# A two-block transformer kernel: small transfers ahead of x, the narrow slab as stationary operand, and input slabs moved between the steps of two attentions

## What is computed

```python
# first block
mod = silu(c) @ w_ada + b_ada            # six vectors of 1024: shifts, scales, gates
h = modulate(rmsnorm(x, norm_mix_g), sh_m, sc_m)
q, k, v, qi, ki, wi, u, ga, gb = split(h @ w_in)    # ki has 64 columns, wi 8
# index scores from qi, ki, wi choose 64 keys for each query; attention over these;
# a gated causal convolution of u (31 taps, w_dw); both projected, gated, added; feed-forward
# second block
h = rmsnorm(x, norm_mix_g)
qa, ka, va, qb, kb, vb, ga, gb = split(h @ w_in_2)  # 512 columns each, ga and gb 1024
qa, ka = rope(qa), rope(ka)
ya = diff_attention(qa, ka, va, lam)     # 4 heads, two softmaxes, second subtracted with lam
yb = chunk_band_attention(qb, kb, vb, rel_bias)     # 8 heads
x = x + (sigmoid(ga) * (ya @ w_up_a) + sigmoid(gb) * (yb @ w_up_b)) @ w_out
# cross attention: q = h @ w_cq, k, v = split(rmsnorm(mem) @ w_ckv); then feed-forward
```

## Time and profile before

| | us |
|---|---|
| median of 3 runs | 979.19 (978.38 to 985.32) |
| the profiled execution | 981.8, its span 980.0 |
| TensorE busy | 932.3 (95%) |
| VectorE, ScalarE, GpSimd busy | 629.6, 458.5, 29.6 |

### The profile page before, as it was taken

The page is one execution under the profiler, slowest core; times in us unless marked ns, Lnnn a source line. Parts: engine busy times, 40 slices in busy tenths (PEclk is TensorE's granted clock), DMA queues, the critical chain, the costliest instruction groups (busy, mean ns, idle before and its releaser), DMA issues.

```text
span 980.0 us, 12127 instructions
## 1 busy us (share of the span) xinstructions
PE 932.3 (95%) x4313; PEld 749.4 (76%) x4313; DVE 629.6 (64%) x1020; ACT 458.5 (47%) x708; POOL 29.6 (3%) x41
## 2 busy tenths in 40 slices
PE   4799899999999999999999999999999999999997
PEld 4688664578878888887888777788788878888785
DVE  4478899988765555576766534578554565555444
ACT  1144432357364444453744554474455365555432
POOL 2100000000000000000000000000000000000000
PEclk9989999999999999999999999999999999999999
DMA  9977622584566565476565443146462456555531
GB/s 330 338 285 271 216 87 87 174 305 175 168 220 210 172 189 196 171 244 228 164 217 177 129 129 129 43 150 216 143 202 85 130 181 194 183 174 194 188 130 43
DMA packets 102999, 178.05 MB, mean 182 GB/s; under 512 B 6302, under 2 KB 52619, under 8 KB 102954
## 3 DMA queue, kind: packets, MB, share of 16 engines
q1 hardware_dynamic: 96138, 151.23, 46.9%
q0 software_dynamic: 6816, 26.22, 7.3%
HBM read 176.39 MB, written 1.05 MB: 181 GB/s over the span
## 4 chain that ended last, share of the span: by engine, by line
PE 81%; issue 7%; DVE 5%; DMA 3%; ACT 2%; SPq 0%; POOL 0%; DVEq 0%; POOLq 0%; ACTq 0%
PE bank L550 19%; PE bank L552 19%; PE bank L551 19%; PE bank L952 10%; PE bank L583 3%; DMA tap_rows<-in_w_dw 2%; DMA ada_raw<-in_w_ada 2%; PE bank L777 1%; ACT w_hi L1201 1%; DVE w_lo L1660 1%; PE bank L931 1%; PE bank L629 1%; PE bank L793 1%; PE bank L621 1%; PE bank L1146 1%
## 5 line engine op out<-in xcount | busy, mean ns | idle before, releaser
L1660 DVE TENSOR_TENSOR w_lo<-raw_weights,w_hi 128x1024 fp32r<-128x1024 f32 x267 | 324.4, 1222 | 241.5 <-ACT w_hi L1201 240.1
L1201 ACT ACTIVATE w_hi<-raw_weights 128x1024 fp32r<-128x1024 f32 x267 | 281.0, 1058 | 307.7 <-PE bank L552 230.0
L550 PE MATMUL bank<-w_hi,a_hi 128*128 128x512 f32 (+1 forms) x824 | 328.0, 398 | 5.9 <-DVE w_lo L1660 3.3
L552 PE MATMUL bank<-w_hi,a_lo 128*128 128x512 f32 (+1 forms) x824 | 321.0, 390 | 0.0
L551 PE MATMUL bank<-w_lo,a_hi 128*128 128x512 f32 (+1 forms) x824 | 320.6, 389 | 0.0
L550 PEld LDWEIGHTS bank<-w_hi,a_hi 128*128 128x128 f32 x824 | 155.6, 189 | 43.4 <-issue 7.3
L552 PEld LDWEIGHTS bank<-w_hi,a_lo 128*128 128x128 f32 x824 | 155.7, 189 | 32.7
L551 PEld LDWEIGHTS bank<-w_lo,a_hi 128*128 128x128 f32 x824 | 155.9, 189 | 29.9 <-issue 0.2
L952 PE MATMUL bank<-w_hi,ff_hi 128*128 128x512 f32 x176 | 55.1, 394 | 0.8 <-DVE hidden_rows L2162 0.5
L952 PE MATMUL bank<-w_lo,ff_hi 128*128 128x512 f32 x176 | 54.3, 389 | 0.0
L952 PE MATMUL bank<-w_hi,ff_lo 128*128 128x512 f32 x176 | 54.2, 389 | 0.0
(11 more groups left out here) (260 smaller groups left out, 867.4 us busy)
## 6 DMA issues: line engine op xcount, KB each, us to landing
raw_weights<-in_w_in SPq DMA_DIRECT2D x40, 1024.0 KB, 5.1
raw_weights<-in_w_ffn_in SPq DMA_DIRECT2D x44, 512.0 KB, 4.7
raw_weights<-in_w_gate_up SPq DMA_DIRECT2D x44, 512.0 KB, 4.3
ada_raw<-in_w_ada POOLq DMA_DIRECT2D x10, 1024.0 KB, 7.7
ada_start<-in_w_ada POOLq DMA_DIRECT2D x10, 1024.0 KB, 11.5
raw_weights<-in_w_ffn_out SPq DMA_DIRECT2D x9, 1024.0 KB, 4.9
raw_weights<-in_w_down SPq DMA_DIRECT2D x9, 1024.0 KB, 4.9
raw_weights<-in_w_out SPq DMA_DIRECT2D x8, 1024.0 KB, 5.1
```

Source lines behind the costliest of these rows:

```text
L550: pe.matmul(ps, hi[:, kt, ts], wh, start=start, stop=False)
L552: return pe.matmul(ps, lo[:, kt, ts], wh, start=False, stop=stop)
L1201: act.activation(w_hi[:, slot, 0:m], raw[:, b % RAW, half * PIECE:half * PIECE + m], ACT.Copy)\
L1660: dve.tensor_tensor(w_lo[:, slot, 0:m], raw[:, b % RAW, half * PIECE:half * PIECE + m], w_hi[:, slot, 0:m], ALU.subtract).then_inc(lo_read ...
```

## The change

SP issues the constants and the small vectors ahead of the wait and of x. TensorE transposes the vectors behind block 1's columns instead of behind the first sums; VectorE copies them behind block 2. The narrow slab's weights become the stationary operand (72 columns) and the rows the moving one (256 columns), so that ki comes out transposed: 24 matmuls. ScalarE evicts it into `kiT`, a DMA on POOL's queue doubles it, and wi is transposed back by TensorE (8 columns a tile). In the second block three slabs (QB, KB, VB) run before banded attention; QA, KA, VA and half of the memory keys run one piece a step in it, and the four gate slabs two pieces a step in differential attention, whose filler is gone. The piece now stands ahead of `d_turn`, ScalarE's eviction ahead of `d_exp`. Rope is cut into four parts in banded attention's steps, its transposes follow in steps 9, 10, 13 and 14, and the transposes of the second half of the memory keys move behind the first query slab. The diff, cut to its core:

```diff
-IN2_COLS = (E_QA, E_KA, E_QB, E_KB, E_VA, E_VB, E_GA, E_GA + W, E_GB, E_GB + W)
+IN2_COLS = (E_QB, E_KB, E_VB)
-MIXED = (("k", 1), ("a", 0), ("a", 1), ("b", 0), ("b", 1), ("v", 0))
-FILL2 = (1,) * 16 + (1, 0) * 4
-AHEAD2 = (0,) * 2 + (1,) * 13 + (0,) + (1, 0) * 3 + (1, 1)
+MIXED = (("h", E_QA), ("h", E_KA), ("h", E_VA), ("k", W), ("h", E_GA), ("h", E_GA + W), ("h", E_GB), ("h", E_GB + W),
+         ("v", 0))
+FILL2 = (1,) * 16 + (2,) * 8
+AHEAD2 = (0,) * 2 + (1,) * 14 + (2,) * 8
+ROPE_AT = {5: ((0, 0),), 6: ((0, 1), (0, 2)), 7: ((1, 0),), 8: ((1, 1), (1, 2)),
+           9: ((2, 0),), 10: ((2, 1), (2, 2)), 11: ((3, 0),), 12: ((3, 1), (3, 2))}
+TURN_AT = (9, 10, 13, 14)
...
-        sp.wait_ge(*ada_signal(1))
-        sp.dma_start(x[:], a["x"].rearrange("o (t p) d -> p (o t) d", p=P)).then_inc(sem["x_landed"], 16)
         early = cols["half"][1]
...
         sp.dma_start(tap_rows[:], a["w_dw"].rearrange("o t i c -> (o t i) c")).then_inc(small_landed, 16)
+        sp.wait_ge(*ada_signal(1))
+        sp.dma_start(x[:], a["x"].rearrange("o (t p) d -> p (o t) d", p=P)).then_inc(sem["x_landed"], 16)
...
-        for n in range(12, 20):
+        for n in range(12, 14):
+            ada_block(n)
+        pool.wait_ge(sem["wi_turned"], 1)
+        pool.dma_start(kiT[DH:2 * DH, :], kiT[0:DH, :]).then_inc(sem["ki_doubled"], 16)
+        for n in range(14, 20):
             ada_block(n)
...
-        for n in range(4):
+        for n in range(2):
             start_columns(n)
         pe.wait_ge(sem["const_landed"], 16)
-        start_sums(0)
-        start_sums(1)
...
         last.then_inc(sem["vec_turned"], 1)
+        for n in range(2, 4):
+            start_columns(n)
+        start_sums(0)
+        start_sums(1)
         hold(5, 0)
...
-        for t in range(TT):
-            for kt in range(KD):
-                last = mm3(bank[2 * (U_SMALL % 2) + t][:, 0:SMALL], kt, t, a_hi, a_lo, sm_hi[:, kt, :],
-                           sm_lo[:, kt, :], kt == 0, kt == KD - 1)
...
+        out = bank[2 * (U_SMALL % 2)][0:SMALL, 0:SEQ]
+        for kt in range(KD):
+            pe.matmul(out, sm_hi[:, kt, :], a_hi[:, kt, :], start=(kt == 0), stop=False)
+            before = pe.matmul(out, sm_lo[:, kt, :], a_hi[:, kt, :], start=False, stop=False)
+            last = pe.matmul(out, sm_hi[:, kt, :], a_lo[:, kt, :], start=False, stop=(kt == KD - 1))
...
+        slab(P_IN2, U_IN2, 0, N_M2)
+        for t in range(TT):
+            pe.wait_ge(acc_free[t], U_K0 + 1)
+        turn4(4, 0, k0_rows, sem["key_turned"])
+        slab(P_IN2 + 4, U_IN2 + 1)
+        for j in range(3):
+            piece(P_IN2 + 8 + j, U_IN2 + 2, j, 4)
+            if j == 0:
                 for t in range(TT):
-                    pe.wait_ge(acc_free[t], U_K0 + 1)
-                turn4(4, 0, k0_rows, sem["key_turned"])
...
+                    pe.wait_ge(acc_free[t], U_IN2 + 2)
                 pe.wait_ge(sem["key_copied"], 2)
...
         for n in range(len(DS)):
-            if n == 0:
-                hold(4, 6)
-            elif n % 2 == 0:
-                for _ in range(9):
-                    pe.matmul(bank[n // 6][:, 3 * P:4 * P], ident, ones, start=True, stop=True)
+            mixed_step(16 + n)
             d_turn(n)
             if n + 2 < len(DS):
                 d_scores(n + 2)
-            mixed_step(16 + n)
...
-        for s in range(2):
-            slab(P_CQ + 4 * s, U_CQ + s, 0, (N_CR) if s == 0 else None)
+        slab(P_CQ, U_CQ, 0, N_CR)
+        for t in range(TT):
+            pe.wait_ge(acc_free[t], U_IN2 + 7)
+        turn4(4, W, k_rows, sem["key_turned"])
+        slab(P_CQ + 4, U_CQ + 1)
...
             keys = P * (n % 2 + 1)
+            mixed_out(16 + n)
             if n + 1 < 8:
                 d_exp(n + 1)
-            mixed_out(16 + n)
             mixed_weights(16 + n)
...
-            elif n == 6:
+            elif n == 2:
                 dve.wait_ge(sem["vec_turned"], 1)
```

More of the change, by code:

```diff
@@ L454, in _ @@
             load(62 + j, slab_src(w2["w_ckv_2"], 4 * j, 0))
-        for s, c in enumerate(IN2_COLS[:6]):
+        for s, c in enumerate(IN2_COLS):
             for j in range(2):
                 load(64 + 2 * s + j, slab_src(w2["w_in_2"], 4 * j, c))
-        first = {"k": 0, "v": D, "a": E_GA, "b": E_GB}
         for m, (kind, c) in enumerate(MIXED):
             for j in range(2):
-                load(76 + 2 * m + j, slab_src(w2["w_ckv_2" if kind in "kv" else "w_in_2"], 4 * j, first[kind] + c * W))
+                load(70 + 2 * m + j, slab_src(w2["w_in_2" if kind == "h" else "w_ckv_2"], 4 * j, c + D * (kind == "v")))
         for n, name in ((88, "w_up_b_2"), (90, "w_up_a_2")):
@@ L1000, in _ @@
             piece(P_K0 + j, U_K0, j, 4, hi=mem_hi, lo=mem_lo, freed_by=(acc_free[0], U_K0))
-        for s in range(4):
-            slab(P_IN2 + 4 * s, U_IN2 + s, 0, N_M2 if s == 0 else None)
-            if s == 1:
-                for t in range(TT):
-                    pe.wait_ge(acc_free[t], U_K0 + 1)
-                turn4(4, 0, k0_rows, sem["key_turned"])
-        for j in range(4):
-            piece(P_IN2 + 16 + j, U_IN2 + 4, j, 4)
-            if j == 1:
-                pe.wait_ge(sem["key_copied"], 2)
[L1011 to L1018, removed]
+        slab(P_IN2, U_IN2, 0, N_M2)
[6 more added lines that the diff above has]
+            if j == 0:
+                for t in range(TT):
+                    pe.wait_ge(acc_free[t], U_IN2 + 2)
+                pe.wait_ge(sem["key_copied"], 2)
                 turn4(4, E_QB, z, sem["t2"])
                 turn4(6, E_KB, z, sem["t2"])
-        pe.wait_ge(sem["t2_copied_act"], 4)
-        pe.wait_ge(sem["t2_copied_dve"], 4)
+        pe.wait_ge(sem["t2_copied_act"], 2)
+        pe.wait_ge(sem["t2_copied_dve"], 2)
         def last_input_piece(scores):
@@ L1027, in last_input_piece @@
             scores(1)
-            piece(P_IN2 + 23, U_IN2 + 5, 3, 4)
+            piece(P_IN2 + 11, U_IN2 + 2, 3, 4)
         def mixed_piece(j):
-            hi, lo = (mem_hi, mem_lo) if MIXED[j // 4][0] in "kv" else (a_hi, a_lo)
-            piece(P_IN2 + 24 + j, U_IN2 + 6 + j // 4, j % 4, 4, pair=1, hi=hi, lo=lo)
+            hi, lo = (a_hi, a_lo) if MIXED[j // 4][0] == "h" else (mem_hi, mem_lo)
+            piece(P_IN2 + 12 + j, U_IN2 + 3 + j // 4, j % 4, 4, pair=1, hi=hi, lo=lo)
         def mixed_step(n):
@@ L1296, in project_slabs @@
                 for k in range(4):
-                    if s == 5 and k == 3:
+                    if s == 2 and k == 3:
                         softmax_exp("b_", 0)
@@ L1333, in _ @@
         for t in range(TT):
-            act.wait_ge(*((piece_used, P_SMALL + 1) if t else (acc_done, U_SMALL + 1)))
-            act.activation(z[:, t, C_KI:C_U], bank[2 * (U_SMALL % 2) + t][:, 0:SMALL], ACT.Copy)\
+            act.wait_ge(piece_used, P_SMALL + 1)
+            act.activation(kiT[0:SMALL, t * P:(t + 1) * P], bank[2 * (U_SMALL % 2)][0:SMALL, t * P:(t + 1) * P], ACT.Copy)\
                 .then_inc(acc_free[t], 1)
@@ L2341, in _ @@
                               ALU.mult).then_inc(acc_free[1], 1)
+            if s == 0:
+                for g in (2, 3):
+                    copy_pair(sem["key_turned"], g + 1, mem_kT[:, 2 * g:2 * g + 2, :], 2 + g, sem["key_copied"])
         for g in (1, 3):
```

143 lines of the change are left out of this document (64 added, 79 removed).

## The result

| | before | after |
|---|---|---|
| median of 20 runs | 981.4 us (977.3 to 985.6) | 985.55 us (982.8 to 987.9) |
| ratio after to before | | 1.0043, interval 1.0026 to 1.0061 |
| the profiled execution, its span | 981.8, 980.0 | 983.0, 981.2 |

A forecast was written before the change was run, and what follows sets the result against it. The prediction took TensorE as the bound, with 81% of the chain. Gains of 6.2 at the start and 5.3 at the narrow slab, less 3.6 in the second block, made 7.9: 979.2 to 971.3 us, range 964.5 to 978.

The forecast's parts named there:

- Part three: Second block: pieces moved out of the stretch before banded attention into the attentions, forecast 3.6 us lost, ends 6 gained and 8 lost.
- hand-over terms: Differential attention: TensorE waits for one conversion between pairs of pieces, 2.48 us for even and 3.07 for odd steps.
- Rope's four parts lie in VectorE's idle time: Before differential attention: rope's parts and the moved key transposes cost nothing, or 1 us if either shows.
- the 0.5 for `turn4` ahead of attention: Before attention: turn4 of KB, now one piece behind its slab, costs up to 1.2 us, taken as 0.5.
- Part two: Narrow slab: 24 matmuls of 256 columns replace 48 of 72; TensorE gains 6.1 us, of which 5.3 counts.
- reckoned step by step the glu product starts 5.3 earlier: Behind the narrow slab: VectorE follows TensorE's gain, so the glu product starts 5.3 us earlier beside the new start.
- Part one: Start: small loads ahead of x and reordered queues bring modulation from 46.4 to 40.2, 6.2 us gained.
- Its better end: Start: the most favourable case, 9.6 us gained, with modulation as early as 36.1.
- Rival (a): Start: the clock rises only behind the whole chain, so 2.4 us gained instead of 6.2, 975.1 in all; chance 15%.
- (c): Differential attention: conversions are ready when wanted, hand-overs cost 1.0 each, 10.6 us less, 960.7; chance 14%.
- (d): Differential attention: each step's second piece also waits for late ScalarE high halves, 16.8 us more, 988.1; chance 5%.
- idle in banded attention would prove the working wrong: Banded attention: a sign named beforehand; idle there in the profile after would refute the forecast's working.

## Why the prediction was wrong

The direction was wrong, and two terms of the sum were.

**Part three was mis-sized, 3.6 for 12 to 14.** Its hand-over terms hold: 2.48 and 3.07 were taken for even and odd steps; at full clock a step takes 8.01 and 8.63, less 5.57 for its two pieces 2.4 and 3.1. The first pieces start 3.5 after the first scores (3.4), and 12 pieces moved out are 32.6. What failed is the step "Rope's four parts lie in VectorE's idle time", taken at "nothing, or 1 if either shows". I read TensorE's idle time for a question about a queue: what stands behind VectorE's maximum is ScalarE's exponential, and behind it the eviction that a slab's first piece waits for. This gave 3.65 of waiting where 0 was taken. And the sum had no term for the clock. I had its fall down to the narrow matmuls alone, and costed waits of 1 to 2 us as waits only. The trace of before had a fall elsewhere that I did not look for, of 3.41 us at 148.09, with a wait of 2.09 just ahead:

```profile
148.03 0.40 PE L786 MATMUL bank<-constants,probabilities 128*128 128x128 f32 x1 [2.09 <-ACT probabilities L1289]
```

It cost nothing there (from this row to the first piece of banded attention 404.8 us with it and 404.8 without it, in the kernel with the new start), since TensorE did not set the pace. In the two attentions of the second block the waits brought four falls in the profiled execution, one at about 1.6 and three at 1.53, 1.60 and 1.62 (9.54, 10.23 and 9.63 for steps of 8.01, 8.63 and 8.01): 6.4. Four turns of q and k in banded attention's steps instead of two of keys, and the key transposes behind the query slab, cost 0.9 each, where nothing was taken. The stretch ahead of attention in turn is shorter by 0.9 more than its 12 pieces: from the glu product to the first piece of banded attention it takes 468.2 in before and 434.7 in the kernel with the second block alone, 33.5 less; that the turns of q and k which moved out are this 0.9 is argued, not shown. The sum: 3.6 forecast, and 3.7 for waits, 6.4 for the clock, 1.8 for transposes, less this 0.9, less 1.6 by which differential attention at full clock (71.2 - 4.75 = 66.4) is shorter than its 68.0, less the 0.5 for `turn4` ahead of attention, which can't be seen: 12.5. The profiled executions have 6.3 + 38.9 + 0.9 - 33.5 = 12.6; the medians had 13.6 for the second block alone.

**Part two, 5.3 for 2 to 3.** TensorE's side came as forecast (24 matmuls in 2.8, no fall behind them). The step that failed is "reckoned step by step the glu product starts 5.3 earlier": VectorE's products start with a block that lands when it lands, 3.93 us of waiting at 61.77, and TensorE gave back 3.07 of it at L703. In the medians nothing of the slab can be seen beside the new start (973.0 and 972.9), though their intervals leave room for 2; in the profiled executions the stretch from modulation to banded attention is 2.8 shorter with it (503.7 and 506.5).

**Part one was right in size, by luck in one step.** 6.2 forecast; 5.5 by the medians and 5.9 by the means of modulation. tap_rows let the transposes start at 18.9, not by 16, and that had no room: TensorE then works without a gap, and in all ten executions with the new start the holds begin 7.8 behind the first transpose (26.66 here). The forecast had them at 26.8 by another path, a late block 3, which TensorE did not wait for behind the transposes; the two errors cancelled. Its better end is also added up wrongly: modulation at 36.1 would be 10.3 gained, not 9.6. That tap_rows goes through one engine agrees with the trace of before, where its packets of 2 KB run one at a time, 0.25 us apart from 25.37 on; but by the section cited in the prediction what counts is a number up to 16 that divides 31, not a divisor shared with 16. Rival (a) asked whether the clock rises only behind the chain: it rises at no fixed place in it, in either order. That the turn is slow in seven executions and fast in seven, slow in the one of before and fast in the one after, is why one profile of each kernel gave 9.4. I had taken the 4.64 of the holds and the 3.51 of the turn in one execution as properties of the order.

**Rivals.** (c), hidden steps, is what the kernel becomes when the conversions stand ahead of the maxima: 10.6 forecast, 12.6 measured with the clock's part of 3.2. (d) put the slower outcome on ScalarE's second piece; at 988.1 its number was near, its mechanism did not occur: no step of TensorE waited for `w_hi`. The 3% stood for slower by more than 9.8 us; the 4 measured lie in "same", which had 0.67, but beyond the range, whose upper end of 978 left no room for slower at all. That came from asking for one such mechanism as (d), when waits of one to two microseconds and the clock behind them were enough. Of the signs named beforehand, "idle in banded attention would prove the working wrong" was the one that decided.

## What to carry to other kernels

Before work is put into an engine's idle time, follow the queue behind it to the next eviction: a step is late by what stands ahead of it in three queues, not by how busy they are. Where work is put between the steps of an attention, evictions and conversions that TensorE needs next go ahead of maxima and exponentials that are wanted a step later; here three moved operations turned +13.6 us into -8.3. Cost a wait of 1 to 2 us of TensorE as itself and, as the worse case, plus a fall of the clock (1.6 here where TensorE sets the pace), and never size a stretch that lies at half clock from one execution.

## What the runs showed of the hardware

The granted clock fell to 0.50 for 3.4 us (at times for 6.83, as from 574.83 in the kernel that evicts first) behind or within short waits of TensorE, but not at all of them. Over the profiles in which each wait occurs:

| wait of TensorE, us | falls at it |
|---|---|
| 2.24, banded attention | 6 of 6 |
| 1.41, banded attention | 0 of 6 |
| 1.09, first piece of differential attention, with 0.81 shortly ahead | 8 of 8 |
| 1.75 and the first 1.60, hand-overs | 3 of 4 and 4 of 4 |
| later 1.60 and 1.11, hand-overs | 1 of 8 and 0 of 8 |
| 1.36, ahead of banded attention | 4 of 14 |
| 0.81 without the 1.09 | 2 of 6 |
| 2.1, attention of the first block | 7 of 14 |
| 1.31, twice behind the second block's attentions | 4 of 28 |
| 1.2, 1.2 and 1.5, ahead of `modulation_T`, `a_lo` and the turn of `scaled_rows` | 0 of 42 |
| 0.66 to 0.71, beside four products of filler | 0 of 4 |

- Filler in the waits kept the clock up at the first two hand-overs, in both kernels that have it. What decides among waits of one length no run here separates. A fall costs about 1.6 us where TensorE sets the pace, and nothing at 148 in before.
- In the start the holds and the turn run at half speed (0.44 us from start to start for 256 columns, later 0.22) until the first record of the granted clock, ahead of which the views print 1.00. When they speed up differs by 3 us and more between executions of one order: the turn takes 1.94 or about 3.5. The Trainium skill ("TensorE: Matmul & The Clock Gate", Part 4) says that transposes do not engage the full clock; where it rose ahead of the turn, the transposes ran at full speed, 0.11 us apart for each of the 16 turned tiles, so 1.9 us of them do not bring it down. Whether they raise it no run here separates.
- A filler of 9 products of 128 columns is 18 records and holds TensorE for 1.93 us.
